# First the second mixer's output of tokens 0-127, then their cross attention; tokens 128-255 among the first head's sums; a smaller DMA scratch and another set of gather buffers

## The chip, the cores and the metric

The kernel runs on one core of a Trainium2 chip. The metric is the device time of one execution, the median of several runs. The engines are named as in the profile: PE is the matrix engine (PEld its weight loads), DVE the vector engine, ACT the scalar engine, POOL is GpSimd, which issues the gathers, and SP issues most weight loads.

## The reference, cut to what matters

One forward pass over 256 tokens of width 1024: a first block (mixer with a gated recurrence and pooling, then a squared-ReLU feed-forward), and a second block, of which the last three steps matter here:

```python
x = x + merged @ w_out[l]                       # output of the second mixer ("wo2")
h = rmsnorm(x, norm_xa_g[l])
m = rmsnorm(mem, norm_mem_g[l])
x = x + memory_cross_attention(h, m, ...)       # query "xq", 4 heads of 128 over 256 memory rows, output "xo"
h = rmsnorm(x, norm_ffn_g[l])
x = x + peer_ffn(h, ...)                        # below
return rmsnorm(x, final_g)

# peer_ffn, for each token and each of 8 heads:
q = xc @ w_q                                    # "pq"
s = einsum("thpd,hpnd->thpn", q, subkeys)       # two lists of 128 scores
# top 16 of each, top 16 of the 256 sums, softmax -> 16 experts e and weights g
a = gelu(einsum("td,thkd->thk", xc, w_down[e]))
y = einsum("thk,thkd->td", g * a, w_up[e])
```

All data are fp32. Each expert has a row of 2048 numbers (its down row and its up row side by side, 8 KB). For 128 tokens and one pick that is a gather of 128 rows, 1.05 MB. There are 8 heads x 16 picks x 2 token halves = 256 gathers.

## The kernel before, in words

Everything is held in SBUF; the weights come from HBM in blocks of 1 MB (`raw`, four slots in turn, `load`, line 542). Accuracy is kept by splitting both operands of a product in two fp32r parts: ACT makes the upper half (`w_hi`, line 1243), DVE the lower (`w_lo`, line 1774), and PE adds three products. Where a product is not split, PE takes fp32 operands directly, as two instructions each. DVE, ACT, PE, SP and POOL each run a program of their own that is written out by hand in order, tied together by semaphores; nothing reorders them.

The work is cut in two halves of 128 tokens, m = 0 (tokens 0-127) and m = 1 (128-255). From the end of the second mixer on, PE's program is:

- `both_sides` (line 1068): first 512 columns of the output, both halves of the tokens; `side_half` (line 1041): the last 512 columns, tokens 0-127, then 128-255 in four pieces among what follows;
- `turn_side` (line 1080): the rows, times the norm's gain, turned for the next product; `cross_query` (line 1095), `cross_scores` (1113), `cross_turn` (1121), `cross_values` (1132), `side` for the cross output (1041), for one half of the tokens and then the other;
- `query` (line 674) and `head_scores` (line 689) of the first head for tokens 0-127;
- the rest of the cross attention of 128-255 and further heads;
- then passes of `sums` (line 1190), one pass for each head and token half, 16 passes in all: a pass holds 16 picks in 8 pairs, and for each pick PE adds the gathered up rows times a diagonal matrix of coefficients. Other heads' queries and scores stand between the pairs of passes 1 to 6.

DVE finds each head's experts (the first pass in pieces: the first pick, seven more, eight more; lines 2515 to 2557), takes the dot product of each gathered down row with the normed tokens (`dot_rows`, line 2564), and makes the coefficients (`coefs`, 2573) out of what ACT's Gelu left (`activate`, 1633 and `DIAG`, 1645). POOL issues the gathers in the order of the picks (line 2778). Before each it waits until the buffer is free: `OPENED` (line 293) says which buffers open when a stage of the cross attention or the queries is over, all other gathers reuse the buffer of an earlier pick when PE has summed it (`up_done`). SP's queue loads the query weights that have a place of their own (`PQW`, line 566) once the merged rows are ready.

## Time and profile before

| | us |
|---|---|
| median of 3 runs | 1303.98 |
| lowest, highest | 1303.90, 1305.43 |
| span of the profiled execution (first to last instruction) | 1302.2 |
| PE busy | 1188.0 (91 %) |
| DVE busy | 920.6 (71 %) |
| ACT busy | 545.5 (42 %) |
| POOL busy | 285.0 (22 %) |
| read from HBM | 394.67 MB, of which gathers 268.45 MB |

The profiled execution's own time is known by its span alone; the median of the runs lies 1.8 us above it. A busy PE is one with matmuls under way, not one at its peak. The slices of the page show which part of the span has which limit, and the chain of waits shows what released what at the end.

### The profile page before, as it was taken

What the parts mean: (1) busy time and instruction counts of PE and PEld (TensorE: products, weight loads), DVE (VectorE), ACT (ScalarE), POOL (GpSimd) and SP (SyncE); (2) the same over time, 40 slices, a digit from 0 to 9 for tenths busy, and PEclk for the clock granted to TensorE, in tenths of its full rate; (3) what the DMA queues carried; (4) which work ended last, traced back from release to release, by engine and by line L of the source; (5) the groups of instructions that cost most, each with busy time, mean ns of one, the idle gap of its engine ahead of it and who ended that gap; (6) DMA issues with size and microseconds to landing.
All of it is one profiled execution on the core that took longest, in us unless ns stands there. A gap on an engine that the chain in (4) does not pass through costs nothing.

```text
span 1302.2 us, 16734 instructions
## 1 busy us (share of the span) xinstructions
PE 1188.0 (91%) x5950; PEld 845.7 (65%) x5950; DVE 920.6 (71%) x1836; ACT 545.5 (42%) x983; POOL 285.0 (22%) x261
## 2 busy tenths in 40 slices
PE   9999999999999999999999889999777877777776
PEld 9998999888888999998865545545322332332322
DVE  6885858777854865567797777776767777777655
ACT  5833655566533547536643333322322222222312
POOL 0000000000000000000145455443643444544420
PEclk9999999999999999999999999999999999989999
DMA  7544456455655654456799999999999999999996
GB/s 287 194 166 148 167 200 213 169 178 183 225 195 194 213 176 160 164 196 230 318 408 402 420 419 420 419 420 419 420 420 418 421 419 422 419 422 419 420 420 262
DMA packets 55925, 396.67 MB, mean 305 GB/s; under 512 B 6320, under 2 KB 6320, under 8 KB 8624
## 3 DMA queue, kind: packets, MB, share of 16 engines
q0 software_dynamic: 36864, 268.45, 49.9%
q1 hardware_dynamic: 17136, 119.16, 25.6%
q10 hardware_dynamic: 1856, 8.13, 1.8%
q8 instruction: 45, 0.74, 0.2%
q14 instruction: 24, 0.20, 0.0%
HBM read 394.67 MB, written 1.05 MB: 304 GB/s over the span
## 4 chain that ended last, share of the span: by engine, by line
PE 56%; DMA 31%; DVE 6%; issue 3%; ACT 3%; POOL 2%; DVEq 0%; POOLq 0%; ACTq 0%
DMA R<-experts,IDX 31%; PE ps L606 19%; PE ps L707 10%; PE ps L1190 8%; PE ps L926 4%; PE ps L654 3%; PE ps L928 2%; POOL R L2778 2%; PE ps L618 2%; DVE R L2564 2%; PE ps L674 1%; PE ps L1041 1%; PE ps L1095 1%; ACT DIAG L1645 1%; PE ps L1068 1%
## 5 line engine op out<-in xcount | busy, mean ns | idle before, releaser
L1190 PE MATMUL ps<-R,DIAG 128*128 128x512 f32 x1020 | 484.6, 623 | 102.7 <-ACT DIAG L1645 97.5
L1190 PEld LDWEIGHTS ps<-R,DIAG 128*128 128x128 f32 x1020 | 191.5, 197 | 371.3 <-issue 206.9
L2564 DVE CUSTOM_DVE_ANT_0 R<-R,XN 128x1024 f32<-128x1024 f32 x256 | 313.4, 1227 | 143.5 <-DMA R<-experts,IDX 137.8
L2778 POOL DMA_INDIRECT R<-experts,IDX x256 | 283.7, 1108 | 535.4 <-PE ps L1190 278.4
L1774 DVE TENSOR_TENSOR w_lo<-raw,w_hi 128x1024 fp32r<-128x1024 f32 x204 | 241.7, 1220 | 89.3 <-ACT w_hi L1243 84.9
L1243 ACT ACTIVATE w_hi<-raw 128x1024 fp32r<-128x1024 f32 x203 | 204.7, 1051 | 78.0 <-DMA raw<-weights 78.0
L1633 ACT ACTIVATE act_d<-dots,rst 128x2 f32<-128x2 f32 (+1 forms) x130 | 38.5, 296 | 329.4 <-DVE dots L2564 329.2
L1645 ACT ACTIVATE DIAG<-con,coef 128x128 f32<-128x128 f32 x255 | 88.6, 394 | 121.3 <-DVE coef L2573 118.1
L606 PE MATMUL ps<-both_C,w_hi 128*128 128x256 f32 x576 | 105.3, 284 | 0.3 <-ACT GA L1277 0.3
L2758 POOL TENSOR_SCALAR_AFFINE_SELECT WS<-WS 128x1024 f32<-128x1024 f32 x1 | 1.1, 1085 | 439.0 <-DMA BS<-gbs 439.0
L606 PEld LDWEIGHTS ps<-both_C,w_hi 128*128 128x128 f32 x576 | 90.3, 192 | 1.4 <-issue 0.8
L606 PE MATMUL ps<-opA_lo,w_hi 128*128 128x256 f32 x320 | 91.1, 285 | 0.1
L926 PE MATMUL ps<-both_C,w_hi 128*128 128x512 f32 x256 | 90.7, 400 | 0.5 <-DVE both_C L1744 0.5
L606 PE MATMUL ps<-opA_hi,w_hi 128*128 128x256 f32 x320 | 90.6, 283 | 0.0
L606 PE MATMUL ps<-opA_hi,w_lo 128*128 128x256 f32 x320 | 90.6, 283 | 0.0
L606 PE MATMUL ps<-both_C,w_lo 128*128 128x256 f32 x288 | 81.5, 283 | 0.0
L928 PE MATMUL ps<-both_C,w_lo 128*128 128x256 f32 x256 | 71.9, 281 | 0.0
L606 PEld LDWEIGHTS ps<-opA_lo,w_hi 128*128 128x128 f32 x320 | 61.4, 192 | 0.5 <-issue 0.5
L606 PEld LDWEIGHTS ps<-opA_hi,w_lo 128*128 128x128 f32 x320 | 61.4, 192 | 0.0
L606 PEld LDWEIGHTS ps<-opA_hi,w_hi 128*128 128x128 f32 x320 | 61.4, 192 | 0.0
L926 PEld LDWEIGHTS ps<-both_C,w_hi 128*128 128x128 f32 x256 | 48.1, 188 | 12.6 <-issue 0.8
L606 PEld LDWEIGHTS ps<-both_C,w_lo 128*128 128x128 f32 x288 | 55.3, 192 | 0.0
(407 smaller groups left out, 1734.2 us busy)
## 6 DMA issues: line engine op xcount, KB each, us to landing
raw<-weights SPq DMA_DIRECT2D x103, 1024.0 KB, 4.8
PQW<-weights SPq DMA_DIRECT2D x6, 1024.0 KB, 9.4
R<-experts,IDX POOLq DMA_INDIRECT x256, 31.8
LNR<-rows ACTq DMA_DIRECT2D x3, 1024.0 KB, 4.7
raw<-weights SPq DMA_DIRECT2D x4, 512.0 KB, 8.4
XF<-xT SPq DMA_DIRECT2D x2, 512.0 KB, 5.6
MEM<-mem ACTq DMA_DIRECT2D x1, 1024.0 KB, 5.0
XR<-x ACTq DMA_DIRECT2D x1, 1024.0 KB, 7.8
```

The costliest lines, as they stand in the source:

```text
L606: mm = pe.matmul(dst[:, c * T:(c + 1) * T], a[:, i, c * P:(c + 1) * P], b[:, k0 + i, :], start=(first and c == 0 and i == ks[0] and n == 0 ...
L654: mm = pe.matmul(bank(r), o[:, 4 * k + i, m * P:(m + 1) * P], a[:, 2 * i:2 * i + 2, :].rearrange("p a b -> p (a b)"), start=(k == 0 and i ...
L707: mm = pe.matmul(psum[:, 4 + 2 * g + m, :], o[:, 4 * k + i, m * P:(m + 1) * P], a[:, 2 * i:2 * i + 2, :].rearrange("p a b -> p (a b)"), st ...
L926: pe.matmul(dst[:, c, :], w_up[:, k, c * P:(c + 1) * P], both_C[:, :, k, :], start=(k == 0), stop=False, skip_group_check=True)
L928: mm = pe.matmul(dst[:, c, 0:T], w_down[:, k, c * P:(c + 1) * P], both_C[:, 0, k, :], start=False, stop=(k == 7), skip_group_check=True)
L1190: mm = pe.matmul(psum[:, 4 + 2 * m + n, :], DIAG[:, k, :], rows_[:, D + n * 512:D + (n + 1) * 512], start=(it % 8 == 0 and k == 0), stop=True,
L1243: act.activation(w_hi[s][:, 4 * h:4 * h + 4, :], raw[s][:, 4 * h:4 * h + 4, :], ACT.Copy).then_inc(hi_ready, 1)
L1633: act.activation(act_d[:, par, k0:k1], dots[:, par, k0:k1], ACT.Gelu_apprx_tanh, scale=rst[:, it // 8:it // 8 + 1]).then_inc(gelu_done, 1)
L1645: ins = act.activation(DIAG[:, k, :], ident, ACT.Copy, scale=coef[:, par, k:k + 1])
L1774: dve.tensor_tensor(w_lo[w][:, ks, :], raw[w][:, ks, :], w_hi[w][:, ks, :], ALU.subtract).then_inc(lo_ready, 1)
L2564: dve.tensor_tensor_reduce(out=rows_[:, 0:D], in0=rows_[:, 0:D], in1=XN[:, m, :], scale=1.0, scalar=0.0, op0=ALU.mult, op1=ALU.add, accum_ ...
L2778: pool.indirect_dma_start(out=R[u][:, :], out_offset=None, in_=experts, in_offset=bass.IndirectOffsetOnAxis(ap=IDX[:, it, k:k + 1], axis=0 ...
```

## The change

In words:

- The second mixer's output for tokens 0-127 (all 1024 columns) comes first. Its first two weight blocks have places of their own (`early_raw`, `early_hi`, `early_lo`), are loaded and split while the stages before run. The output of tokens 128-255 follows in 16 pieces (`second`) among the cross attention of tokens 0-127.
- The cross attention of 0-127 keeps split products. That of 128-255 (query, output) is done in plain fp32 from the unsplit blocks (`XQ`, `XO`), after the first head's scores; its turns, values and output stand among the sums of the first pass. The queries of heads 2 and 3 move there too.
- The norm's gains of the cross attention and the feed-forward are applied per partition when turned rows leave PSUM (four 128-wide instructions instead of one of 512 for tokens 0-127), so rows are turned before the gain. The 1/rms goes into the softmax's scale. The rows with gains that the dot products need are made by `gain_side` between the first and the second eight picks.
- The first head's query is made in pieces as the turned rows arrive, and its two halves leave PSUM apart.
- All eight query blocks have a place (`PQW`) and are loaded by SP at new points.
- The scratch of the DMA descriptors is 4096 bytes per partition instead of the default 16384. The room gives more places for tiles; 17 buffers serve for gathers, as before, but five of them open with the cross output of tokens 0-127, two with the second cross query, one with its values, two with its output.

```diff
+DMA_SCRATCH = 4096
@@ the order of queries
-QUERIES = [(0, 0), (1, 0), (2, 0), (3, 0), (0, 1), (4, 0), (1, 1), (5, 0), (2, 1), (6, 0), (3, 1), (7, 0),
+QUERIES = [(0, 0), (1, 0), (2, 0), (3, 0), (4, 0), (0, 1), (5, 0), (1, 1), (6, 0), (2, 1), (7, 0), (3, 1),
...
@@ gather buffers
-        OPENED = {0: (11, None), 1: (18, None), 2: (8, VALUES_END)}
-        for n, u in enumerate((s0, 4 + s0)):
-            OPENED[3 + n] = (u, FIRST_XO_END)
-        for n, u in enumerate((s0 + 1, 5 + s0, 12)):
-            OPENED[5 + n] = (u, XO_END)
-        for n, u, j in ((21, 3, 0), (34, 0, 1), (51, 14, 2), (68, 15, 3), (85, 7, 4), (93, 4, 5), (101, 9, 6),
-                        (109, 13, 7), (110, 10, 7)):
+        OPENED = {0: (18, ("xo_a", 3)), 1: (5, ("xo_a", 3)), 2: (6, ("xo_a", 3)), 3: (22, ("xo_a", 3)),
+                  4: (24, ("xo_a", 3)), 5: (1, ("xq_b", 1)), 6: (2, ("xq_b", 1)), 9: (8, ("values", 1)),
+                  14: (14, ("xo_b", 2)), 15: (15, ("xo_b", 2))}
+        for n, u, j in ((36, 9, 0), (52, 11, 1), (69, 3, 2), (86, 7, 3), (96, 0, 4), (104, 4, 5), (114, 12, 6)):
@@ SP's queue
+            load(ma + 1, slot_of(ma + 1), half_end(ma - 3))
+            whole(early_raw[0], wo2, early_in[0])
+            load(gm, slot_of(gm), half_end(ma - 2))
+            sp.wait_ge(gm_ready, 2)
+            whole(early_raw[1], wo2 + 1, early_in[1])
+            load(gm + 1, slot_of(gm + 1), half_end(ma - 1))
+            load(wo2 + 2, slot_of(wo2 + 2), half_end(ma))
+            load(wo2 + 3, slot_of(wo2 + 3), half_end(ma + 1))
+            for n in range(2):
+                sp.wait_ge(gemm_done, half_end(gm + n))
+                whole(XQ[n], xq + n, xq_in[n])
             sp.wait_ge(m2_ready, 4)
...
+            for b, js in ((wo2, (1,)), (wo2 + 2, (2, 3)), (wo2 + 3, (4, 5, 6, 7))):
+                sp.wait_ge(gemm_done, half_end(b))
+                for j in js:
+                    whole(PQW[j], PQ0 + j, pq_in[j])
@@ PE, up to the first head's scores
+            for i in range(8):
+                wo2_rows(0, 0, i)
+            for i in range(4):
+                wo2_rows(1, 0, i)
+            turn("h3Ta", 0, "wo2", 1, XR, 0, range(4))
+            for i in range(4, 8):
+                wo2_rows(1, 0, i)
+            cross_query(0, 0)
+            turn("h3Ta", 1, "wo2", 2, XR, 0, range(4, 8))
+            cross_query(0, 1)
+            cross_query(1, 0)
+            cross_query(1, 1)
+            second(1)
...
+            second(1)
+            cross_scores(0, 0)
+            cross_scores(0, 1)
+            second(6)
+            cross_turn(0, 0)
+            second(2)
+            cross_turn(0, 1)
+            second(4)
+            cross_values(0)
+            turn("h3Tb", 0, "wo2", 3, XR, 1, range(4))
+            second(2)
+            has_lo(pe, "ax", 0)
+            cross_out(0)
+            cross_out(1, slice(0, 256))
...
+            turn("h3Tc", 0, "wo2", 4, XR, 1, range(4, 8))
+            head_scores(0, 0)
+            cross_query_second()
+            cross_scores(1, 0)
+            cross_scores(1, 1)
+            query(1, 0)
             head_scores(1, 0)
@@ PE, the first pass of sums
             sums(0, 0)
+            cross_turn(1, 0)
+            cross_turn(1, 1)
             sums(0, 1)
-            query(3, 0, (1,))
+            cross_values(1)
             sums(0, 2)
+            wait_aux(pe, "xpvb")
+            cross_out_second(0)
+            sums(0, 3)
+            cross_out_second(1)
+            sums(0, 4)
+            query(2, 0)
+            sums(0, 5)
+            head_scores(2, 0)
+            query(3, 0)
+            sums(0, 6)
             head_scores(3, 0)
...
@@ DVE, from the first head's scores
             first_eight()
-            values_lo(1)
             inverse_side(3, 0)
+            dve.wait_ge(rows2_in, 32)
+            gain_side(0, first_cols)
+            gain_side(0, last_cols)
             second_eight()
+            cross_max(1, 0)
+            cross_max(1, 1)
             top_h(0)
-
+            dve.wait_ge(xn_gain, 2)
+            dot_rows(0, 0)
+            coefs(0, 0)
+            cross_weights(1, 0)
+            cross_weights(1, 1)
+            dot_rows(0, 1)
+            coefs(0, 1)
             top_a(1)
+            dot_rows(0, 2)
+            coefs(0, 2)
             top_b(1)
...
+            dot_rows(0, 3)
+            residual_side("xo", 4, 1, first_cols)
+            coefs(0, 3)
@@ the program's start
-    nc = bacc.Bacc("TRN2", target_bir_lowering=False, num_devices=1)
+    nc = bacc.Bacc("TRN2", target_bir_lowering=False, num_devices=1, dynamic_dma_scratch_size=DMA_SCRATCH)
```

The order on three engines, before and after. PE around the first head's scores (`SK` are the subkeys, `QP` the turned query, `XS` the softmax weights of the cross attention). Before:

```order
L1113 MATMUL ps<-KX,QX 128x256
L1113 MATMUL ps<-KX,QX 128x256 [waits aux_drained0,drained1,wide_drained]
L1113 MATMUL ps<-KX,QX 128x256
L1080 MATMUL ps<-con,XN 128x128 [waits xn_gain,wide_drained]
L1080 MATMUL ps<-con,XN 128x128 x3
L674 MATMUL ps<-H_133,raw_54 128x128 [waits aux_drained1,raw_ready3,drained0]
L674 MATMUL ps<-H_133,raw_54 128x128 x7
L674 MATMUL ps<-H_133,raw_54 128x128 [waits aux_drained0]
L674 MATMUL ps<-H_133,raw_54 128x128 x7
L1121 MATMUL ps<-con,XS 128x128 [waits att_p]
L1121 MATMUL ps<-con,XS 128x128 x3
L689 MATMUL ps<-SK,QP 128x128 [waits aux_drained1,sk_in,drained0]
```

The same place after:

```order
L691 MATMUL ps<-H4A,PQW_155 128x128 [waits aux_drained1]
L691 MATMUL ps<-H4A,PQW_155 128x128 x3
L1097 MATMUL ps<-con,XR 128x128 [waits wide_drained,aux_drained0]
L1097 MATMUL ps<-con,XR 128x128 x3
L719 MATMUL ps<-SK,QP 128x128 [waits aux_drained1,first_query,sk_in]
L719 MATMUL ps<-SK,QP 128x128 [waits drained0]
L1128 MATMUL ps<-H3B,XQ_147 128x128 [waits aux_drained0,xq_in0,drained1]
L1128 MATMUL ps<-H3B,XQ_147 128x128 x3
L1128 MATMUL ps<-H3B,XQ_148 128x128 [waits xq_in1]
L1128 MATMUL ps<-H3B,XQ_148 128x128 x3
```

The cross scores of tokens 128-255 (`QX`) stood ahead of the first head's scores; now even their query (L1128) comes behind them.

PE in the first pass, around the third pair of sums (`R` are gathered rows). Before:

```order
L1190 MATMUL ps<-R_148,DIAG 128x512 [waits row_in5,dg_ready]
L1190 MATMUL ps<-R_148,DIAG 128x512
L1190 MATMUL ps<-R_145,DIAG 128x512 [waits row_in2]
L1190 MATMUL ps<-R_145,DIAG 128x512
L689 MATMUL ps<-SK,QP 128x128 [waits aux_drained1,drained1]
L689 MATMUL ps<-SK,QP 128x128
L1190 MATMUL ps<-R_149,DIAG 128x512 [waits row_in6,dg_ready]
L1190 MATMUL ps<-R_149,DIAG 128x512
```

After:

```order
L1160 MATMUL ps<-XT,VX 128x128 [waits xt_second,att_t,aux_drained1,drained0,drained1]
L1160 MATMUL ps<-XT,VX 128x128 x7
L1247 MATMUL ps<-R_182,DIAG 128x512 [waits row_in24,dg_ready]
L1247 MATMUL ps<-R_182,DIAG 128x512
L1247 MATMUL ps<-R_167,DIAG 128x512 [waits row_in1]
L1247 MATMUL ps<-R_167,DIAG 128x512
L1181 MATMUL ps<-XO_149,AXB 128x512 [waits xo_in0,aux_drained1]
L1181 MATMUL ps<-XO_149,AXB 128x512 x3
L1247 MATMUL ps<-R_168,DIAG 128x512 [waits row_in2,dg_ready]
L1247 MATMUL ps<-R_168,DIAG 128x512
```

Values (L1160) and output (L1181) of the second tokens' cross attention now stand between the pairs.

POOL, the first ten gathers. Before:

```order
L2778 DMA R_154<-experts,IDX 128x2048 [waits idx_ready]
L2778 DMA R_159<-experts,IDX 128x2048 [waits idx_ready]
L2778 DMA R_151<-experts,IDX 128x2048 [waits aux_done]
L2778 DMA R_144<-experts,IDX 128x2048 [waits gemm_done]
L2778 DMA R_148<-experts,IDX 128x2048 [waits gemm_done]
L2778 DMA R_145<-experts,IDX 128x2048 [waits gemm_done]
L2778 DMA R_149<-experts,IDX 128x2048 [waits gemm_done]
L2778 DMA R_155<-experts,IDX 128x2048 [waits gemm_done]
L2778 DMA R_154<-experts,IDX 128x2048 [waits up_done,idx_ready]
L2778 DMA R_151<-experts,IDX 128x2048 [waits up_done]
```

After:

```order
L2923 DMA R_180<-experts,IDX 128x2048 [waits xo_a,idx_ready]
L2923 DMA R_171<-experts,IDX 128x2048 [waits xo_a,idx_ready]
L2923 DMA R_172<-experts,IDX 128x2048 [waits xo_a]
L2923 DMA R_181<-experts,IDX 128x2048 [waits xo_a]
L2923 DMA R_182<-experts,IDX 128x2048 [waits xo_a]
L2923 DMA R_167<-experts,IDX 128x2048 [waits xq_b]
L2923 DMA R_168<-experts,IDX 128x2048 [waits xq_b]
L2923 DMA R_171<-experts,IDX 128x2048 [waits up_done]
L2923 DMA R_172<-experts,IDX 128x2048 [waits up_done,idx_ready]
L2923 DMA R_174<-experts,IDX 128x2048 [waits aux_done]
```

The first wait for a sum (`up_done`) stood at the ninth gather and stands at the eighth.

## Rows read from the trace of the kernel before

**Rows 1.** The page: busy time of each engine, and GB/s in its 40 slices.

```profile
PE 1188.0 (91%) x5950; PEld 845.7 (65%) x5950; DVE 920.6 (71%) x1836; ACT 545.5 (42%) x983; POOL 285.0 (22%) x261
...
GB/s 287 194 166 148 167 200 213 169 178 183 225 195 194 213 176 160 164 196 230 318 408 402 420 419 420 419 420 419 420 420 418 421 419 422 419 422 419 420 420 262
```

**Rows 2.** Busy time by stretch: length, engines' busy us, PE clock, DMA share, GB/s.

```profile
642.50:645.00 2.50, 2.50 (x25) 2.50 (x24) 2.26 (x15) 1.23 (x4) 1.14 (x2) 1.00 0.34 62
645.00:647.50 2.50, 2.03 (x17) 1.81 (x16) 2.27 (x12) 0.49 (x2) 1.79 (x2) 1.00 0.96 383
...
642.50:700.00 57.50, 54.36 (x250) 35.22 (x249) 49.62 (x161) 23.35 (x57) 27.79 (x25) 1.00 0.97 385
700.00:1285.00 585.00, 485.81 (x1330) 222.59 (x1328) 414.64 (x1072) 167.16 (x431) 255.93 (x232) 0.96 1.01 420
1285.00:1293.20 8.20, 7.40 (x17) 3.23 (x18) 4.20 (x10) 2.78 (x8) 0.00 (x0) 1.00 0.32 131
```

**Rows 3.** The chain that ended last, in order of time: start us, us, what.

```profile
585.85 10.93 PE ps L1068 x48
...
683.73 3.44 PE ps L1190 x8
...
1258.83 34.33 DMA R<-experts,IDX
...
1293.18 1.23 DVE R L2564
```

**Rows 4.** Timeline of POOL: start us, us, line, operation [idle before, releaser].

```profile
642.48 1.09 POOL L2778 DMA_INDIRECT R<-experts,IDX  x1 [201.91 <-DVE IDX L2523]
644.92 0.94 POOL L2778 DMA_INDIRECT R<-experts,IDX  x1 [1.36 <-DVE IDX L2470]
646.16 0.94 POOL L2778 DMA_INDIRECT R<-experts,IDX  x1 [0.31 <-issue]
...
661.59 0.95 POOL L2778 DMA_INDIRECT R<-experts,IDX  x1 [4.68 <-PE ps L1190]
...
690.94 1.82 POOL L2778 DMA_INDIRECT R<-experts,IDX  x1 [1.97 <-PE ps L1190]
```

**Rows 5.** Timeline of DVE.

```profile
564.52 2.36 DVE L1774 TENSOR_TENSOR w_lo<-raw,w_hi 128x1024 fp32r<-128x1024 f32 x2 [3.23 <-ACT w_hi L1243]
...
640.50 0.50 DVE L2515 MAX8 tv<-ps 128x8 f32<-128x128 f32 x2 [1.70 <-PE ps L689]
...
644.48 0.17 DVE L2470 SCALAR_TENSOR_TENSOR IDX<-ef 128x7 uint32<-128x7 f32 x1
...
651.39 0.17 DVE L2470 SCALAR_TENSOR_TENSOR IDX<-ef 128x8 uint32<-128x8 f32 x1
...
654.87 1.23 DVE L2564 CUSTOM_DVE_ANT_0 R<-R,XN 128x1024 f32<-128x1024 f32 x1
```

**Rows 6.** Timeline of PE.

```profile
585.69 0.40 PE L1068 MATMUL ps<-w_hi,both_C 128*128 128x512 f32 x1
...
632.71 1.97 PE L1113 MATMUL ps<-KX,QX 128*128 128x256 f32 x8 [0.34 <-ACT QX L1552]
...
640.74 1.95 PE L674 MATMUL ps<-H,raw 128*128 128x128 f32 x16
642.52 1.95 PE L1132 MATMUL ps<-XT,VX 128*128 128x128 f32 x16
...
658.83 7.13 PE L1190 MATMUL ps<-R,DIAG 128*128 128x512 f32 x16
```

**Rows 7.** Timeline of ACT.

```profile
596.70 1.28 ACT L1422 ACT_TABLE_LOAD   x1
...
598.23 0.63 ACT L1524 ACTIVATE XS<-XR 128x512 f32<-128x512 f32 x1
...
658.08 0.70 ACT L1645 ACTIVATE DIAG<-con,coef 128x128 f32<-128x128 f32 x2
```

**Rows 8.** The gathers' issue line: POOL's durations in ns, min/median/max.

```profile
L2778 POOL DMA_INDIRECT R<-experts,IDX x256: 932/937/1985, 642.5 to 1258.8; - x128
```

More of the change, by code:

```diff
@@ L659, in by_rows, with query_part @@
                             mm.then_inc(gemm_done, 1)
+            def query_part(j, m, c, ks):
+                r = RING["pq"] + QUERIES.index((j, m))
+                apart = (j, m) == (0, 0) and c == 1
+                dst = bank(r + 1 if apart else r)[:, c * P:(c + 1) * P]
+                for k in ks:
+                    mm = pe.matmul(dst, PQW[j][:, k, c * P:(c + 1) * P], H4[m][:, k, :],
+                                   start=((c == 0 or apart) and k == 0), stop=(k == 7), skip_group_check=True)
+                return mm
@@ new lines, in _, with second, turn @@
+            second_rows = iter([(g, i) for g in range(2) for i in range(8)])
+            def second(count):
+                for _ in range(count):
+                    g, i = next(second_rows)
+                    wo2_rows(g, 1, i)
+            def turn(name, j, stage, n, src, m, chunks):
+                dst = free_aux(name, j)
+                wait_wide(pe, stage, n)
+                for n_, c in enumerate(chunks):
+                    mm = pe.transpose(dst[:, n_ * P:(n_ + 1) * P], src[:, m, c * P:(c + 1) * P], ident)
+                mm.then_inc(aux_done, 1)
@@ new lines, in cross_query_second @@
+            def cross_query_second():
+                r = RING["xq"] + 1
+                free_bank(r)
+                wait_aux(pe, "h3Tb")
+                wait_aux(pe, "h3Tc")
+                for h in range(XH):
+                    for k in range(DC):
+                        if h == 0 and k % 4 == 0:
+                            pe.wait_ge(xq_in[k // 4], 16)
+                        at_ = 2 * (k % 4) + h // 2
+                        mm = pe.matmul(bank(r)[:, h * P:(h + 1) * P],
+                                       XQ[k // 4][:, at_, (h % 2) * P:(h % 2 + 1) * P], H3B[:, k, :],
+                                       start=(h == 0 and k == 0), stop=(k == 7), skip_group_check=True)
+                mm.then_inc(xq_b, 1)
@@ new lines, in cross_out_second @@
+            def cross_out_second(g):
+                pe.wait_ge(xo_in[g], 16)
+                for i in range(4):
+                    mm = pe.matmul(psum[:, 6 + g, :], AXB[:, i, :],
+                                   XO[g][:, 2 * i:2 * i + 2, :].rearrange("p a b -> p (a b)"),
+                                   start=(i == 0), stop=(i == 3), skip_group_check=True)
+                mm.then_inc(xo_b, 1)
+            for i in range(8):
+                wo2_rows(0, 0, i)
+            for i in range(4):
+                wo2_rows(1, 0, i)
@@ L1150, in _ @@
+            turn("h3Ta", 0, "wo2", 1, XR, 0, range(4))
[7 more added lines that the diff above has]
+            second(1)
+            wait_drained(pe, "xq", 0)
+            transposes("qTa", 0, [QN[:, h * P:(h + 1) * P] for h in range(XH)])
+            second(1)
             cross_scores(0, 0)
```

766 lines of the change are left out of this document (389 added, 377 removed).

## The prediction

> **What bounds the kernel now.** I read the page's slices first, then the busy time by stretch, then the chain of waits, then the timelines of each engine around the place that the chain points to. The slices show two halves [rows 1]. In the first twenty of 40 slices 150 to 320 GB/s flow; from slice 21 it is 400 and then about 420 until the end. These are the gathers of expert rows, 256 of 128 rows of 8 KB. By stretch: from 700 to 1285 us the share is 1.01 at 420 GB/s [rows 2]. So a gather of 1.05 MB costs 1.05/0.420 = 2.50 us there, and 256 of them 640 us, whatever the compute engines do. The chain says the same: 34.33 us of DMA lie between the last gather's issue (1258.83) and the last dot product (1293.18), and 9 us follow to the end at 1302.2 [rows 3].
>
> The time is therefore: when the first gather starts, plus how long the DMA engines run dry, plus 640 us, plus a tail. The first gather is issued at 642.48 [rows 4], 1.98 us after VectorE starts on the first head's scores at 640.50 [rows 5]. From 642.5 to 700 us the mean is 385 GB/s, so (420-385) x 57.5 / 420 = 4.8 us are lost there; about half of it is the latency of the very first gather: by 647.5 only (62 + 383) x 2.5 = 1.11 MB had come, 2.65 us of full flow, so flow in effect began 2.4 us after the issue [rows 2]. After 1285 the DMA engines empty unevenly (131 GB/s over 8.2 us): some 5.5 us of tail, the same in both kernels.
>
> **What the change moves: the way to the first gather.** On PE, second-mixer output starts at 585.7 [rows 6]. Before, everything of tokens 128-255 up to its cross-attention scores stands ahead of the first head's scores, 54.8 us later. Costs from the rows: a 128x512 fp32r matmul 10.93/48 = 0.228 us [rows 3]; 16 fp32 instructions of 128x128 1.78 us, so a query projection (32 of them) 3.56 and a values product (16) 1.78 [rows 6]; four transposes about 0.35; an fp32 128x256 pair 0.47 (cross scores of four heads, eight instructions, 1.9 us) [rows 6]. After, ahead of the first head's scores stand: output of tokens 0-127, 48 matmuls, 10.9; its query, 24, 5.5; output of 128-255, 48, 10.9; cross scores 1.9; turns of the weights 0.7; values 1.8; cross output of 0-127, 12 wide and 24 of half width, 5.5; query projection 3.6; head scores 0.4; transposes, some 24, 2.5. Sum 43.7 us. The difference is what the change leaves for later: half of the cross query (5.5, replaced later by 32 fp32 matmuls, 7.1), cross scores 1.9 and one turn of 0.35, and part of the overheads.
>
> PE will wait on this path, because tokens 128-255 no longer fill the gaps. I went through the three engines step by step with the durations of [rows 5 and 7]. ScalarE does the table load (1.28), the square (0.8) and four scaled 128x128 copies at 0.35 instead of one of 512 before PE may use the normed rows: PE waits about 0.6, then 0.9 for the second half; copying and turning the cross query about 0.7; the two-step copy of the first query about 0.4. Sum 2.6 us. The rest (softmax, 0.9 us VectorE steps, the weights' halves at 1.2 us each) is hidden behind the sixteen pieces of the second tokens' output, 0.68 us each. So VectorE starts on the scores at 585.7 + 43.7 + 2.6 = 632.0 instead of 640.5: **8.5 us earlier**, first gather at 634.0.
>
> Upstream: the halves of two output blocks are split ahead, while the stages before run. That is 4.0 us more ScalarE and 4.7 us more VectorE work between 557 and 577 us, where VectorE stands idle 3.23 us before one row alone [rows 5]; I find room for all of it, and drains at most 1.3 us late, with PE not waiting. I take 0, bounds 0 and 3. SP's queue now has one load behind a wait for the gated rows of the second mixer (which need only the stage before, while the load behind it waits for a later one anyway) and two cross-query loads behind the last stage; ScalarE waits for one of these ahead of the last upper half, at worst 1 us, inside the same bounds. All query weights are asked for before 621, so 4 MB are in at about 631, ahead of the gathers.
>
> **What it costs: the first pass over the gathered rows.** The buffers open differently. Before, eight gathers need no sum; the ninth is issued at 661.59, after the first sum. After, seven need none (five at once, two after the second cross query at +8); the eighth waits for the second pick's sum. Seven gathers last 17.5 us. When do the sums start? Times from here are after VectorE's start on the scores (640.50 and 632.0). Before, the first sum is at 658.83, so +18.3 [rows 6]. After: VectorE has the first eight picks at +4.7, gains 1.3, the second eight (5.4) at +11.5, two cross maxima 1.7, gate weights 0.5, two dot products 2.3 (two instructions, 2.37 together) at +16 [rows 5]. ScalarE meanwhile has four exponentials behind these maxima, a query copy, the Gelu table (1.28) and a score copy [rows 7], and so activates at +17: first sum at +18.0, second pick at +21.5, eighth gather at +21.9.
>
> Then PE carries, between sums of 3.44 us per pair [rows 3]: two turns 0.7, values 1.8, the cross output of 128-255 as eight fp32 matmuls of 0.86, 6.9, two whole query projections 7.1, two head scores 0.9, two transposes 0.7. With 27.5 for the sums that is 45.6 us, against 40 that sixteen gathers need from the DMA engines, and 34.4 before. And VectorE stands at the wait for the first cross output ahead of the fourth pair's coefficients, which PE must then wait for, 1.6 us. Following it: second pair at +23.0, values done +28.1, third pair from +28.7, cross output done +35.6, fourth pair +37.2 to +40.6, second cross output done at **+44.1**. The fifteenth gather waits for that and nothing later binds more (the closest, six gathers on, has 1.4 us to spare). Into a dry queue a gather takes 2.4 us from issue to full flow, as the first one shows. So the fifteenth flows at 632.0 + 44.1 + 0.4 + 2.4 = 678.9. Before, the last gather that is late is the twentieth, issued at 690.94 [rows 4], flowing at 693.3; the fifteenth, five gathers before it, would have to flow at 693.3 - 12.5 = 680.8. From there both run at 2.50 us per gather, since later passes hold 35.5 us of PE work for 40 of DMA. **Net 680.8 - 678.9 = 1.9 us.** Of the 8.5 us gained ahead, 6.6 are given back as dry queue.
>
> **Issuing.** The smaller scratch: gathers follow each other at 1.25 us when nothing holds them, 0.94 of it busy (644.92, 646.16) [rows 4]. The DMA engines take one per 2.50, so reclaiming space may cost 1.25 us each time before it is seen. No trace shows a small ring; bounds 0 and, if it held back the queue, tens of us. I take 0, because the nearest row, the issue's median of 937 ns over all 256 [rows 8], shows no cost of space on the larger one however often that was reused. The longest issue took 1985 ns [rows 8]. The Trainium skill (SBUF — State Buffer, summary of rules for kernel authors) says that descriptor generation on GpSimd is starved while VectorE is in its faster modes; the change puts VectorE work beside the first gathers. If the fifteenth were slowed to the longest row, the sum would be 1 us later, 1303; I keep the median, and no run here separates the two.
>
> **The rest** costs nothing: final gains loaded once instead of later (off the path), gains of 128-255 moved into a later pass (1.3 us of VectorE, which is 71 % busy [rows 1]).
>
> **How the numbers follow.** Span 1302.2 - 1.9 = 1300.3; the median of the runs, 1303.98, lies 1.8 above the span, so **1302.0**. About 0.2 % (2.6 us) is what a measurement can tell from no change.
>
> - *Forecast*, the gain mostly paid back: 1302.0, own range 1299 to 1305. Chance 0.46.
> - *The early start is kept*: the sums' stages overlap better than I laid out (VectorE not blocked, ScalarE's copies between), so the fifteenth gather is asked for 5 us sooner. Then 1297, and up to 8.5 early, 1295. For it: the total of PE work is smaller by 5 us. Against: seven gathers are 17.5 us and the sums start at +18. Chance 0.27.
> - *Slower: the first pass starves the gathers.* PE's 45.6 us against 40. Every us that the second cross output ends later than +46.0 makes the kernel slower than before; at +51, because VectorE's order or a late landing stalls two pairs, 1307. For it: each later pair sits close behind (1.4 us of room). Chance 0.18.
> - *The earlier stages pay*: the extra halves push the start of the output by 3 us and loads 1 more: 1305 to 1306. Chance 0.05.
> - *The small scratch holds the queue*: issues over 2.5 us; each 0.1 us above gives 24 us. Over 1320. Chance 0.04.
>
> Range 1296 to 1308, which leaves out about 2 in 10. Faster by over 0.2 % (below 1301.4): 0.18 of the forecast and 0.26 of the second, 0.44. Slower (above 1306.6): 0.14 of the starved case, 0.04 scratch, 0.02 of the rest, 0.20. Within: 0.36.
>
> **What the profile would show.** First gather near 634 (640 or later would put the step from 54.8 to 46.3 us wrong). First sum 18 us after the scores. Eighth gather issued near 654, fifteenth near 676.5; between them GB/s clearly under 420, afterwards 420 to the end. PE idle before the fourth pair for a wait on coefficients. Issue spacing 1.25 us where no wait holds it. Wrong would be: dry queue after 700, or a last stage before 585 that ends later.

## The result

Before 1304.18 us (median of 5 runs, 1303.9 to 1305.43), after **1315.27 us** (median of 5, 1309.93 to 1318.68). The ratio is 1.0085, 95% interval 1.007 to 1.010: slower by 11 us, where 1302.0 had been forecast with a range up to 1308. The profiled run of after took 1317.0 us with a span of 1315.2. A second set of runs of the same kernel, beside the experiments, gave 1312.86 us (1308.38 to 1312.97, 5 runs; before 1303.61 there). Its five runs lie in two groups, 1308.4 to 1308.9 and 1312.9 to 1313.0, and their mean is 1311.2, so a difference from that median is good to some 2 us only.

### The profile after

The page: busy time and GB/s in 40 slices of 32.9 us, as [rows 1].

```profile
PE 1190.0 (90%) x5990; PEld 847.0 (64%) x5990; DVE 919.0 (70%) x1838; ACT 545.7 (41%) x997; POOL 285.4 (22%) x261
...
GB/s 285 192 170 151 161 196 221 160 192 190 219 196 195 196 185 152 176 270 213 347 297 316 383 419 420 420 420 419 420 420 419 420 420 420 421 419 421 419 420 271
```

The busy time is the same as before to 2 us on every engine. In [rows 1] 400 GB/s stood from slice 21 on; now slices 20 to 23 show 347, 297, 316 and 383. Time was lost as dry DMA queue (stretches in which the DMA engines had too few gathers to do), and, as the sum below shows, nowhere else to 0.4 us. The busy time by stretch (length, busy us of PE, PEld, DVE, ACT, POOL, granted clock, DMA share, GB/s) says where, first of after:

```profile
635.41:690.00 54.59, 46.74 (x213) 30.66 (x212) 37.11 (x121) 13.80 (x40) 20.31 (x19) 0.94 0.83 311
690.00:740.00 50.00, 43.00 (x165) 24.80 (x166) 35.11 (x107) 21.48 (x55) 15.48 (x15) 0.93 0.86 327
```

and of before, from its first gather on:

```profile
642.48:690.00 47.52, 44.95 (x225) 31.02 (x225) 42.90 (x144) 21.03 (x50) 21.07 (x19) 1.00 0.97 380
690.00:740.00 50.00, 46.48 (x162) 24.46 (x161) 38.48 (x103) 17.15 (x42) 24.54 (x23) 1.00 1.01 418
```

Against a full 420 GB/s after loses (420 - 311) x 54.59 / 420 = 14.2 us up to 690 and 93 x 50 / 420 = 11.1 us from 690 to 740, together 25.3. Before loses 4.5 + 0.2 = 4.8. The first gather goes out at 635.41 instead of 642.48. So 25.3 - 4.8 - 7.1 = 13.4 us are to be expected, and the spans differ by 13.0. This sum of three terms (first issue, lost before 690, lost behind 690) is used for all kernels below.

The timeline of POOL: start, duration, and in brackets the idle time ahead and what ended it. It answers [rows 4].

```profile
635.41 1.08 POOL L2923 DMA_INDIRECT R<-experts,IDX  x1 [194.27 <-DVE IDX L2660]
...
660.10 1.08 POOL L2923 DMA_INDIRECT R<-experts,IDX  x1 [14.81 <-PE ps L1247]
...
681.90 0.94 POOL L2923 DMA_INDIRECT R<-experts,IDX  x1 [3.26 <-PE ps L1181]
...
702.13 1.22 POOL L2923 DMA_INDIRECT R<-experts,IDX  x1 [6.65 <-PE ps L1247]
...
718.07 0.93 POOL L2923 DMA_INDIRECT R<-experts,IDX  x1 [5.60 <-PE ps L1247]
```

The eighth gather (660.10) and the fifteenth (681.90) wait for PE as foreseen, though later. But the 22nd and the 26th too wait for sums (L1247), 6.65 and 5.60 us, where two gathers last 5.0, so the queue runs dry. The prediction had no dry queue behind the fifteenth. PE's timeline, which answers [rows 6], shows why (a pair's sum is eight matmul instructions, L1247):

```profile
643.64 2.80 PE L1141 MATMUL ps<-KX,QXB 128*128 128x256 f32 x8 [1.89 <-issue]
646.24 4.59 PE L691 MATMUL ps<-H4A,PQW 128*128 128x128 f32 x32
...
654.43 5.40 PE L1247 MATMUL ps<-R,DIAG 128*128 128x512 f32 x8 [2.42 <-ACT DIAG L1749]
...
684.90 3.73 PE L691 MATMUL ps<-H4A,PQW 128*128 128x128 f32 x32
690.57 3.70 PE L1247 MATMUL ps<-R,DIAG 128*128 128x512 f32 x8 [1.94 <-ACT DIAG L1749]
...
694.55 3.74 PE L691 MATMUL ps<-H4A,PQW 128*128 128x128 f32 x32
699.87 3.70 PE L1247 MATMUL ps<-R,DIAG 128*128 128x512 f32 x8 [1.58 <-ACT DIAG L1749]
...
705.86 5.40 PE L1247 MATMUL ps<-R,DIAG 128*128 128x512 f32 x8 [1.85 <-ACT DIAG L1749]
...
715.13 5.40 PE L1247 MATMUL ps<-R,DIAG 128*128 128x512 f32 x8 [3.00 <-ACT DIAG L1749]
```

Two things are to be seen. Ahead of each of the last three sums of the first pass and the first of the second, PE waits for ScalarE's diagonals: 1.94 + 1.58 + 1.85 + 3.00 = 8.4 us. And the eight matmuls of a sum take 5.40 us three times instead of 3.6 to 3.7. The granted clock says the latter:

```profile
640.00:644.00 4.00, 2.12 (x18) 1.93 (x17) 3.72 (x20) 0.97 (x3) 3.08 (x4) 1.00 1.00 371
644.00:648.00 4.00, 4.00 (x17) 3.57 (x16) 3.16 (x12) 1.73 (x6) 0.99 (x2) 0.58 0.97 385
...
654.00:658.00 4.00, 3.57 (x5) 1.65 (x6) 3.60 (x9) 0.68 (x3) 0.00 (x0) 0.61 0.55 231
```

It is near 0.5 (1.2 GHz instead of 2.4) in 644 to 648 and in 654 to 658, each time right behind idle time of PE (1.89 and 2.42 us). ScalarE's timeline shows what the diagonals waited for:

```profile
688.96 0.38 ACT L1757 ACTIVATE QP<-ps 128x256 f32<-128x256 f32 x1 [8.72 <-PE ps L691]
689.24 0.29 ACT L1737 ACTIVATE act_d<-dots,rst 128x2 f32<-128x2 f32 x1
689.82 0.69 ACT L1749 ACTIVATE DIAG<-con,coef 128x128 f32<-128x128 f32 x2 [0.30 <-DVE coef L2710]
...
699.83 1.28 ACT L1499 ACT_TABLE_LOAD   x1
...
701.58 1.28 ACT L1729 ACT_TABLE_LOAD   x1
...
703.30 1.28 ACT L1737 ACT_TABLE_LOAD   x1
704.59 0.29 ACT L1737 ACTIVATE act_d<-dots,rst 128x2 f32<-128x2 f32 x1
...
711.73 2.17 ACT L1685 ACTIVATE H4B<-ps,vec 128x128 f32<-128x128 f32 x8 [5.57 <-PE ps L1097]
```

In ScalarE's program the copy of the query (QP) stands ahead of the activation of pair 6. It waits 8.72 us until PE has finished the query, and the activation, whose dot products VectorE had ended 4.5 us before, waits behind it. So PE does sum, query, **wait**, sum, query, wait. Three table loads (ScalarE's changes to another set of functions: root, exponential, Gelu) stand ahead of pair 8's activation, and eight copies of turned rows (2.17 us) ahead of the next. That a root and an exponential bring a load each is also what the Trainium skill says (ScalarE: Activation LUTs, "Table sets: the hidden batching unit": they lie in different sets); this trace agrees. The section puts two such changes at about 5.3 us; here a load takes 1.28 us and the next activation starts at its end (703.30 + 1.28, and 704.59), and the measured figure is the one used.

### The profile page after: what moved, and what is told of

The parts are those of the page before. It is cut to its first block, busy times and chain, and to the rows that moved or that the text cites. A ratio compares the mean times of both kernels' runs of the same rounds, so it can differ in the third digit from the quotient of the medians.

```text
span 1315.2 us, 16824 instructions
## 1 busy us (share of the span) xinstructions
PE 1190.0 (90%) x5990; PEld 847.0 (64%) x5990; DVE 919.0 (70%) x1838; ACT 545.7 (41%) x997; POOL 285.4 (22%) x261
## 3 DMA queue, kind: packets, MB, share of 16 engines
HBM read 394.15 MB, written 1.05 MB: 300 GB/s over the span
## 4 chain that ended last, share of the span: by engine, by line
PE 62%; DMA 30%; DVE 3%; ACT 3%; issue 2%; POOL 1%; DVEq 0%; POOLq 0%; ACTq 0%
DMA R<-experts,IDX 29%; PE ps L630 18%; PE ps L1247 12%; PE ps L737 10%; PE ps L954 4%; PE ps L691 3%; PE ps L678 3%; PE ps L956 2%; PE ps L642 2%; PE ps L1077 1%; ACT DIAG L1749 1%; DVE R L2701 1%; PE ps L773 1%; DMA XQ<-weights 1%; POOL R L2923 1%
## 5 line engine op out<-in xcount | busy, mean ns | idle before, releaser
L1247 PE MATMUL ps<-R,DIAG 128*128 128x512 f32 x1020 | 481.9, 619 | 109.8 <-ACT DIAG L1749 109.6
L1247 PEld LDWEIGHTS ps<-R,DIAG 128*128 128x128 f32 x1020 | 190.2, 196 | 375.3 <-issue 197.0
L1883 DVE TENSOR_TENSOR w_lo<-raw,w_hi 128x1024 fp32r<-128x1024 f32 x192 | 227.4, 1220 | 85.0 <-ACT w_hi L1305 81.1
L1305 ACT ACTIVATE w_hi<-raw 128x1024 fp32r<-128x1024 f32 x191 | 192.8, 1052 | 80.6 <-DMA raw<-weights 79.2
```

The source lines that it names most:

```text
L1247: mm = pe.matmul(psum[:, 4 + 2 * m + n, :], DIAG[:, k, :], rows_[:, D + n * 512:D + (n + 1) * 512], start=(it % 8 == 0 and k == 0), stop=True,
L1305: act.activation(w_hi[s][:, 4 * h:4 * h + 4, :], raw[s][:, 4 * h:4 * h + 4, :], ACT.Copy).then_inc(hi_ready, 1)
L1883: dve.tensor_tensor(w_lo[w][:, ks, :], raw[w][:, ks, :], w_hi[w][:, ks, :], ALU.subtract).then_inc(lo_ready, 1)
```

## The experiments

Three theories. **A**: the order of ScalarE's and VectorE's programs ties the sums to PE's other work. **B**: PE's sheer load in the first pass, 45 us against 40 of gathers. **C**: PE's waits cost twice, through the clock. Besides, the smaller scratch and the cross-query load were to be settled. Each row of the table has one trace, of one of its runs.

| run | edit | median us (runs) | against before, 95% |
|---|---|---|---|
| e1_scratch | before, scratch 4096 | 1303.52 (10) | 0.9992 to 1.0012 |
| e8_after_again | after, unedited | 1312.86 (5) | 1.0034 to 1.0070 |
| e2_act_order | ScalarE's order | 1308.32 (4) | 1.0026 to 1.0060 |
| e3_xq_late | cross-query half later | 1311.94 (4) | 1.0059 to 1.0093 |
| e4_short_out | 5.2 us less on PE | 1306.88 (5) | 1.0021 to 1.0049 |
| e5_fill | filler transposes | 1307.45 (10) | 1.0021 to 1.0040 |
| e9_dve_late | VectorE's two additions later | 1309.52 (4) | 1.0035 to 1.0065 |
| e6_combo | order mended throughout | 1300.67 (9) | 0.9967 to 0.9992 |
| e7_combo_fill | e6 and filler | 1299.47 (6) | 0.9952 to 0.9977 |
| e10_mended_short | e7, 5.2 us less on PE | 1298.16 (4) | 0.9944 to 0.9974 |
| e11_first_sum | e7, one copy later | 1298.58 (5) | 0.9951 to 0.9979 |

### e1_scratch: the scratch alone

```
-    nc = bacc.Bacc("TRN2", target_bir_lowering=False, num_devices=1)
+    nc = bacc.Bacc("TRN2", target_bir_lowering=False, num_devices=1, dynamic_dma_scratch_size=4096)
```

> The kernel before, with the DMA scratch of 4096 bytes as its only edit. If the smaller scratch costs nothing (my first theory; in the changed kernel's trace an issue on GpSimd still takes 932 to 938 ns), the time stays within 0.1% of 1304.2 us and gathers that nothing holds follow each other at 1.25 us. If it is the scratch that costs the 11 us (rival), this kernel takes about 1315 us by itself.

1303.52 us against 1303.49: nothing. The issue line (min/median/max in ns), to be held against [rows 8]:

```profile
L2778 POOL DMA_INDIRECT R<-experts,IDX x256: 935/941/1974, 641.3 to 1257.5; - x128
```

### e3_xq_late: the load that ScalarE waits for

```
                 if j == 2:
-                    upper_cross(XQ, xq_in, 0, 0)
...
+            upper_cross(XQ, xq_in, 0, 0)
             upper_cross(XQ, xq_in, 0, 1)
```

> The changed kernel, with ScalarE's first upper half of the cross-query block moved from ahead of the last upper part of the gated rows to behind it. If PE's 1.4 us at 589.5 is ScalarE waiting for that block's load, PE no longer stops there, the first gather goes out 1.2 to 1.5 us earlier (634.0) and the time falls by 1 to 1.5 us to about 1314. If the wait only moves to the cross query (rival), the first gather stays at 635.4.

In after the chain of waits has this piece (start us, us, what):

```profile
580.33 8.20 DMA XQ<-weights
...
588.55 0.34 ACT cross_hi L1342
...
589.52 0.62 ACT both_C L1365
...
590.17 0.70 DVE both_C L1853
...
591.00 4.37 PE ps L1077 x18
```

PE stands still 0.84 us at 591.00, because a half of the cross query stood ahead of the last gated rows on ScalarE. With the edit the stop is gone and the first gather goes out at 634.20, 1.2 us sooner. From PE's first matmul of the second mixer's output (about 585.9 in both) to VectorE's start on the scores it is 46.3 us instead of 47.5. The median fell by 0.9 us against the later set of after and 3.3 against the first, but its runs (1310.9 to 1314.1) lie among those of after, so only the trace shows the 1.2 us. That start itself lies at 584.3 to 584.4 in the profiled runs of e2, e9, e10 and e11 and at 585.9 to 586.1 in those of the other kernels made from after, which no edit explains, and which shifts everything behind it by 1.6 us.

### e2_act_order: ScalarE's program

```
             activate(0, 4)
-            queries(2, 0)
             activate(0, 5)
             square_side("xo", 5, 1, 1)
+            queries(2, 0)
+            activate(0, 6)
             head_scores(2, 0)
             queries(3, 0)
-            activate(0, 6)
+            activate(0, 7)
             warm(ACT.Sqrt)
             root_side(4, 1)
             gate_exp(1)
-            activate(0, 7)
             head_scores(3, 0)
-            for j in range(2):
-                rows_second(j)
```

The copies rows_second(0) and (1) follow the first and the second activation of the next pass; on VectorE inverse_side(4, 1) stands behind coefs(0, 7).

> The changed kernel, with ScalarE's order in the first pass changed alone: the activations of pairs 6 and 7 stand ahead of the copies of the query projections of heads 2 and 3, the activation of pair 8 ahead of the root and the exponential (three table loads), and the copies of the second tokens' rows behind the activations of pairs 1 and 2 of the next pass. Theory A (ScalarE's order ties each sum to the query ahead of it): PE's idle times ahead of the sums at 686, 697, 704, 711 us (1.94, 1.58, 1.85, 3.00) mostly go, and the sums at full granted clock save another 1 to 2 us each: 6 to 10 us faster than the changed kernel, 1306 to 1309. Theory B (PE's sheer load of 45 us against 40 of gathers): at most 1 us.

1308.32 us, 4.5 to 7 less than after. PE's timeline of this kernel:

```profile
681.34 3.73 PE L691 MATMUL ps<-H4A,PQW 128*128 128x128 f32 x32
684.91 3.60 PE L1247 MATMUL ps<-R,DIAG 128*128 128x512 f32 x8
...
688.79 3.74 PE L691 MATMUL ps<-H4A,PQW 128*128 128x128 f32 x32
692.36 3.60 PE L1247 MATMUL ps<-R,DIAG 128*128 128x512 f32 x8
...
696.24 3.60 PE L1247 MATMUL ps<-R,DIAG 128*128 128x512 f32 x8
...
704.78 6.14 PE L1247 MATMUL ps<-R,DIAG 128*128 128x512 f32 x8 [4.07 <-ACT DIAG L1749]
```

Three of the four waits are gone with not one instruction less (the start of the mixer's output 1.6 us earlier in this run was lost again at the cross-query load: 48.3 us from there to the scores, first gather at 634.55). One has grown to 4.07 us: the three table loads now delay the gate weights of the second head, which VectorE awaits ahead of its next dot products. Behind it the sum takes 6.14 us. Lost from 690 to 740 are (420 - 373) x 50 / 420 = 5.6 us instead of 11.1.

### e4_short_out: less work on PE

```
-                for i in range(4):
+                for i in range(1):
                     mm = pe.matmul(psum[:, 6 + g, :], AXB[:, i, :],
```

> The changed kernel, leaving out three quarters of the second tokens' cross output in the first pass (2 of 8 fp32 matmuls are done), so 5.2 us less work on PE between the second and the fifth pair's sums. Theory B (PE's load): 5 us faster, about 1310, and the DMA engines less dry at once. Theory A (ScalarE's order and the waits later in the pass bind): the fifteenth gather is asked for 5 us sooner, but the idle times ahead of the sums behind the queries stay, and 2 to 4 us are gained.

1306.88 us, 6 to 8 less. It seemed to speak for B, and it is more than the 5.2 us of work removed, so part of it was something else (in its profiled run the first sum took 3.70 us behind the same 2.41 us wait). Its trace up to 690:

```profile
636.03:690.00 53.97, 45.65 (x241) 31.44 (x241) 39.39 (x125) 15.28 (x44) 22.31 (x21) 1.00 0.95 367
```

That is 6.8 us lost, against 11.9 in e8, whose first sum was slow, and 9.8 in e5 (below), whose first sum was not. So with the clock held the lighter load saved up to 3.0 us of dry queue on the changed kernel. e10 repeats the cut where the order is mended.

### e5_fill and e8_after_again: the clock

```
             cross_query_second()
+            filler(10)
             cross_scores(1, 0)
...
+            filler(24)
             sums(0, 0)
```

A filler is a transpose of rows of tokens 0-127 into a bank that the first sum overwrites; nothing reads it.

> The changed kernel with filler work alone: 10 needless transposes ahead of the second cross scores and 24 ahead of the first sum, where PE waits for ScalarE. Theory C (the idle time ahead of the first sum costs twice, since the granted clock falls to 0.50 behind it): the clock stays at 1.00 from 640 to 660, the first sum's eight instructions take 3.6 us instead of 5.40, the eighth gather goes out 22 to 23.5 us after VectorE's start on the scores (26.7 before), and the time falls by 2 to 4 us against the changed kernel, 1311 to 1313. Rival (the sums are late for the order of VectorE and ScalarE alone): no change, or 1 us slower by the filler itself.

> The changed kernel once more, unedited, beside the others of this call: 1310 to 1318 us as before. Its first result spread over 9 us. If that spread comes from the granted clock, the profiled run shows where it fell, and the sums there take 5.4 us or more per pair instead of 3.6.

1307.45 us against 1312.86: **34 needless instructions more, and faster**, by 5.4 us in the medians and 3.5 in the means (1307.7 and 1311.2). First e8's, then e5's clock, stretches and first sum:

```profile
648.00:654.00 6.00, 3.11 (x9) 1.70 (x9) 4.60 (x12) 3.46 (x9) 0.00 (x0) 0.82 1.02 427
635.48:690.00 54.52, 47.45 (x219) 30.47 (x219) 39.23 (x125) 14.93 (x43) 20.45 (x20) 0.97 0.88 328
690.00:740.00 50.00, 43.57 (x180) 26.05 (x179) 35.26 (x106) 20.88 (x53) 16.41 (x16) 0.93 0.90 338
```

```profile
651.81 5.40 PE L1247 MATMUL ps<-R,DIAG 128*128 128x512 f32 x8 [2.41 <-ACT DIAG L1749]
```

```profile
648.00:654.00 6.00, 5.53 (x44) 4.85 (x43) 4.52 (x13) 4.72 (x13) 0.00 (x0) 1.00 1.01 421
636.72:690.00 53.28, 49.46 (x254) 33.56 (x254) 39.24 (x125) 14.84 (x43) 20.62 (x20) 1.00 0.92 343
690.00:740.00 50.00, 43.58 (x187) 26.40 (x186) 37.55 (x114) 21.69 (x55) 19.78 (x18) 1.00 0.94 361
```

```profile
650.48 2.78 PE L1238 MATMUL ps<-con,XR 128*128 128x128 f32 x24
653.10 3.66 PE L1253 MATMUL ps<-R,DIAG 128*128 128x512 f32 x8
```

The eighth gather goes out 22.3 us behind VectorE's start on the scores (657.03 - 634.74) instead of 24.0 (657.48 - 633.50) in e8 and 26.7 (660.10 - 633.43) in the first trace of after. The later waits (1.70, 1.65, 1.58, 1.85, 3.00) are all still there in e5, yet each sum behind them took 3.70 us. In the stretch where the filler stands, up to 690, e5 lost 9.8 us against 11.9. The other 2.8 us (7.0 against 9.8 from 690 to 740) are not the filler's by any row: there the sum behind the 3.00 us wait took 6.75 us in e8 and 3.70 in e5, with no filler near. Without filler, the wait of 2.4 us ahead of the first sum was followed by a slow sum in five of seven kernels' profiled runs (not in e4 and e9); the wait of 3.0 us ahead of the second pass, which no filler touched, in four of six (not in e4 and e5). The fall is thus not certain at such a wait, which is one likely cause of after's spread of 9 us over its runs; the two starts of the mixer's output (1.6 us) and the wait for the cross-query load (46.3 to 48.7 us from there to the scores) are others. Before, whose PE hardly waits there, spreads over 1.5 us in its first set and 2.6 to 3.7 in the later ones. That the unprofiled runs differ in the same way was not shown.

### e9_dve_late: VectorE's residual additions

```
-            residual_side("xo", 4, 1, first_cols)
             coefs(0, 3)
+            residual_side("xo", 4, 1, first_cols)
```

and the same with residual_side("xo", 5, ...) and coefs(0, 5).

> The changed kernel, with nothing but VectorE's two residual additions of the second tokens moved behind the coefficients of pairs 4 and 6. In the changed kernel VectorE waits 5.8 us for the cross output at 667 to 672 us and PE then 1.70 us for the coefficients queued behind it. If that wait is on the path, pair 4 starts 1 to 1.7 us earlier and the fifteenth gather with it: 1 to 2 us faster than the changed kernel (1311 to 1312 against 1312.9). If the waits behind it swallow the gain, no change.

1309.52 us, 3.3 less than after's later set in the medians and 1.8 in the means, with ranges that overlap (1307.12 to 1311.43 and 1308.38 to 1312.97). The fourth pair's sum (665.61) no longer waits, where it waited 1.70; in its place the fifth waits a little:

```profile
673.20 3.70 PE L1247 MATMUL ps<-R,DIAG 128*128 128x512 f32 x8 [0.56 <-ACT DIAG L1749]
```

That explains 1.1 us. Anything beyond it is not this edit's by any row: in the profiled run the clock stayed at 1.00 behind the first sum's wait, and the cross-query load came in time (ScalarE waited 0.35 us for it, not 2.31), which gave 46.3 us up to the scores without e3's edit. How far the other three runs had the same luck was not shown.

### e6_combo, e7_combo_fill: all of it together

e6 joins e3, e2 and e9, and moves gate_exp(1) behind activate(0, 4) and the root behind activate(0, 6), each with its table load back (`warm` runs a function once on one number, so that its set is loaded). That makes four loads ahead of pair 8's activation in place of three; activate(0, 7) now stands behind head 2's scores and head 3's query:

```
             activate(0, 4)
+            gate_exp(1)
+            warm(ACT.Gelu_apprx_tanh)
             activate(0, 5)
             square_side("xo", 5, 1, 1)
             queries(2, 0)
             activate(0, 6)
+            warm(ACT.Sqrt)
+            root_side(4, 1)
+            warm(ACT.Gelu_apprx_tanh)
             head_scores(2, 0)
             queries(3, 0)
             activate(0, 7)
```

> The changed kernel with the order mended everywhere I found a wait: the cross-query half late as in the third run; ScalarE's activations ahead of the query copies as in the second; the exponential of the second head ahead of pair 6, the root behind pair 7, each with its table loads; VectorE's two residual additions of the second tokens behind the coefficients instead of ahead of them. Theory A: the 4.07 us ahead of the first sum of the second pass and the 1.70 us ahead of pair 4 go, 3 to 4 us less than the second run's 1308.3, so 1304 to 1305.5, level with the kernel before. Theory B (PE carries 45 us against 40): stays at 1307 to 1308.

> The sixth run's kernel with the fifth run's filler transposes. If the clock costs 2 to 4 us ahead of the first sum, that comes on top: 1301.5 to 1303.5, a little faster than the kernel before. If not, the same as the sixth.

1300.67 and 1299.47 us: more than expected, and both faster than the kernel before. By stretch, e6 has

```profile
634.34:690.00 55.66, 51.38 (x249) 33.97 (x249) 40.09 (x129) 22.95 (x57) 21.79 (x21) 0.97 0.89 344
690.00:740.00 50.00, 48.77 (x186) 27.47 (x186) 43.95 (x128) 21.10 (x55) 24.85 (x22) 1.00 1.01 419
```

Behind 690 nothing is lost (0.1 us against 11.1). The sum of the three terms is 10.1 + 0.1 - 4.8 - 8.1 = -2.7, and the span is 1299.7, 2.5 below before's. e7 lies 1.2 us lower still, with intervals that overlap. Its trace lost 7.6 us up to 690 against e6's 10.1, a saving in the filler's stretch like that on after (9.8 against 11.9), but 1.4 behind 690 against 0.1, which no row explains.

### e10_mended_short: theory B again

The edit of e4 on e7.

> The seventh run's kernel (order mended, filler in), leaving out three quarters of the second tokens' cross output in the first pass: 5.2 us less work on PE. Between 650 and 680 us the seventh run still loses 4.1 us of full flow, (70 + 61 + 42) x 10 / 420. Theory B (what is left is PE's load): 2 to 4 us faster, about 1296. Theory A (only waits counted): no change from 1299.5. Either way the gain is smaller than the 6 us that the same cut gave the changed kernel (1312.9 to 1306.9), if part of that came from waits.

1298.16 us, 1.3 less than e7, for the same 5.2 us of work that seemed to be worth 6 on after. Even that is not clear of the spreads (1296.19 to 1300.1 and 1297.46 to 1301.33), and the profiled run's first gather goes out 2.0 us earlier than e7's (632.77 and 634.77), since it had the earlier start. Its dry queue is 0.6 us less (6.9 + 1.5 against 7.6 + 1.4). PE now reaches the fifth pair 3.13 us before its diagonals, which VectorE and ScalarE can't deliver sooner, and the sum behind is slow:

```profile
670.74 6.65 PE L1253 MATMUL ps<-R,DIAG 128*128 128x512 f32 x8 [3.13 <-ACT DIAG L1755]
```

So theory B brought little once the order was right. One thing stays open: the slow sum took 3.0 us more than e7's fifth (3.70), and what the lighter load would have saved with the clock held was not measured.

### e11_first_sum: the best found

```
             warm(ACT.Gelu_apprx_tanh)
-            head_scores(1, 0)
             activate(0, 0)
+            head_scores(1, 0)
...
-            filler(24)
+            filler(20)
```

> The seventh run's kernel, with ScalarE's copy of the second head's scores behind the first activation and four filler transposes fewer. ScalarE's copy is 0.47 us ahead of the first Gelu; the first sum should start 0.4 us sooner and the time fall by 0.3 to 0.5 us to about 1299. Within what a measurement can tell it may well be the same as the seventh, 1299.5; it should again be faster than the kernel before by 3 to 5 us.

1298.58 us (1297.52 to 1301.07), ratio to before 0.9965, 95% interval 0.9951 to 0.9979. The first sum stands 17.96 us behind the scores (648.63 - 630.67) against 18.37 in e7: the 0.4 us are there in the trace, but against e7's median the gain is within the spread. Like the profiled runs of e2, e9 and e10, this one had the earlier start: its first gather goes out 2.1 us before e7's, and its span is 2.0 us shorter. By stretch:

```profile
632.65:690.00 57.35, 56.32 (x294) 38.59 (x294) 43.26 (x139) 23.55 (x59) 21.60 (x22) 1.00 0.94 362
690.00:740.00 50.00, 48.77 (x189) 27.68 (x188) 43.59 (x125) 20.73 (x54) 26.85 (x24) 1.00 1.01 419
```

The account (us), all from such rows:

| | first issue, against 642.48 | lost before 690 | lost 690 to 740 | sum, less 4.8 | span, against 1302.2 |
|---|---|---|---|---|---|
| after | -7.1 | 14.2 | 11.1 | +13.4 | +13.0 |
| e8, after again | -7.0 | 11.9 | 9.8 | +9.9 | +8.8 |
| e3, cross-query half later | -8.3 | 11.4 | 9.2 | +7.5 | +6.9 |
| e2, ScalarE's order | -7.9 | 11.5 | 5.6 | +4.4 | +4.2 |
| e4, 5.2 us less on PE | -6.5 | 6.8 | 8.5 | +4.0 | +2.9 |
| e9, VectorE's additions later | -9.8 | 8.5 | 10.6 | +4.5 | +3.2 |
| e5, filler | -5.8 | 9.8 | 7.0 | +6.2 | +5.7 |
| e6, order mended | -8.1 | 10.1 | 0.1 | -2.7 | -2.5 |
| e7, e6 and filler | -7.7 | 7.6 | 1.4 | -3.5 | -4.5 |
| e10, e7 with less on PE | -9.7 | 6.9 | 1.5 | -6.0 | -6.1 |
| e11, best | -9.8 | 7.9 | 0.1 | -6.6 | -6.5 |

## Why the prediction was wrong

**What bounds the kernel**: right. The tail of 420 GB/s is unchanged, and all differences are first issue plus dry queue, to 1.3 us at worst (e9). The span missed by 14.9 us (1315.2 against 1300.3): 11.1 of them are dry queue behind 690, where none was forecast, 1.4 the later first issue, and the rest dry queue before 690.

**The way to the first gather**: right in its sum (43.7 + 2.6 = 46.3 us from the output's start to the scores), wrong in one bound. The kernels with e3's edit show 46.3 to 46.8, the others 46.3 (e9, where the load came in time) to 48.7 (e5), after itself 47.5 and 47.6: the wait for the cross-query load, bounded "at worst 1 us" and taken as 0, put 1.2 on the way, and up to 2.4 in e5. First issue 635.4 instead of 634.0.

**The first sums**: +18.0 was right for a full clock (+18.3 in e8 and e9, +18.4 in e5). It was +21.0 in the first trace of after, 2.7 us later than in e8: 1.7 since the cross scores and the query ran at the lower clock (2.80 and 4.59 us instead of 1.97 and 3.73), and 1.0 since PE had stood still 1.89 us ahead of these scores instead of 0.84 (e8), which no row explains. The eighth gather, forecast at +21.9, came at +22.3 with the clock held (e5), at +24.0 and +26.7 without. No term of the sum stood for the clock. [rows 2] showed it at 1.00 up to 700, but on a PE that stood idle 3 us in 57 (and at 0.96 behind, where PE is less busy); the change opened waits, and the full clock was carried over unasked.

**The second cross output**: forecast done at +44.1; e5, with the clock held, shows +43.8 (678.50, where the next sum starts, less 634.74), and the predicted stop ahead of the fourth pair (1.6 us) measures 1.70. First trace: +48.0.

**The net of 1.9 us** has a slip. It lets the twentieth gather of before flow 2.4 us after its issue at 690.94, as into a dry queue. By the stretch from 642.48 to 690.94 (48.46 us at 381 GB/s) 18.5 MB had come, at most 17.6 gathers of 1.05 MB, and 19 had been issued. So 1.4 or more were still under way, 3.5 us of flow, and by this estimate it flowed at 694.4, not 693.3: a net of 3.0 us. The slip made the forecast 1.1 us too slow and explains nothing of the miss.

**The step that failed** is the sentence "nothing later binds more (the closest, six gathers on, has 1.4 us to spare)". The prediction names steps of VectorE and ScalarE up to the fourth pair's coefficients; from pair 5 on it counts PE's work alone and takes their results as ready, so it put these waits at nothing. There ScalarE's program holds the copy of each query ahead of the next activation, three table loads ahead of pair 8 and eight copies ahead of pair 1 of the next pass. They cost 8.4 us of PE's waits, and 11.1 us of dry queue: 7.0 when every sum behind them ran at the full clock (e5), the rest with the slow sums that followed them (9.8 in e8). e6, which differs from after in order and by one table load more, loses 0.1 us there and takes 1300.7, below the forecast of 1302.0. The forecast's mechanism (early start, mostly paid back; 11.4 us lost before 700 in all) holds for that kernel, with 10.1 lost.

**The rivals.** "The first pass starves the gathers" named the right side and the right stretch. Its cause, PE's load, was worth up to 3.0 us of dry queue on the changed kernel (e4 against e5) and 0.6 once the order is mended (e10, with a slow sum in it), so it was a smaller part of the miss than the order. The rival's words "VectorE's order ... stalls two pairs" come nearer. Its chance, 0.18, was too low, for the 1.4 us of room that I had worked out were less than any wait on the two engines that I had not followed. "Earlier stages pay" came true by 1.2 us. "The small scratch" is refuted by e1.

## What to carry to other kernels

When work is moved among the steps of a pipelined loop, follow every in-order engine to the end of the stretch, not only the one with the most work: a short copy that waits for a long step holds up a short step that was ready, and mending such an order took no work away and gave 12 us in the medians, 10 in the means (e8 and e6). Leave room in a forecast for the clock wherever a change opens waits on PE, and where PE must wait, filler may be worth more than it costs. A cut of work that gains more than its own length is no proof of load: try it again once the waits are gone.
